# Memory keys computed during the modulation, and half of the modulation summed on TensorE

## The reference, cut to what matters

```
mod = silu(c) @ ada_w + ada_b            # ada_w: 1024 x 3072; shift, scale, gate
h = rms_norm(x, norm_g) * (1 + scale) + shift
p = h @ w_in                             # RWKV-7 branch and sparse attention follow
x = x + gate * (merged @ w_o); x = rms_norm(x, final_g)
```

```
x = x + rmsnorm(y @ w_out, mix_post_g)           # end of the mixture
h = rmsnorm(x, mem_pre_g)
mem_n = rmsnorm(mem, mem_kv_g)                   # depends on inputs alone
q = h @ w_mq;  k, v = split(mem_n @ w_mkv)       # w_mkv: 1024 x 2048
o = softmax(q k^T / 16) v                        # 4 heads of 256
x = x + rmsnorm(o @ w_mo, mem_post_g)
```

## Time and profile before

| | us |
|---|---|
| median of 3 runs | 1289.8 (1287.19 to 1291.56) |
| the profiled execution | 1291.93 |
| its span in the trace | 1290.1 |

### The profile page before, as it was taken

The page is one execution under the profiler, slowest core; times in us unless marked ns, Lnnn a source line. Parts: engine busy times, 40 slices in busy tenths (PEclk is TensorE's granted clock), DMA queues, the critical chain, the costliest instruction groups (busy, mean ns, idle before and its releaser), DMA issues.

```text
span 1290.1 us, 21180 instructions
## 1 busy us (share of the span) xinstructions
PE 1180.9 (92%) x8372; PEld 997.0 (77%) x8372; DVE 467.7 (36%) x833; ACT 593.4 (46%) x869; POOL 905.7 (70%) x913
## 2 busy tenths in 40 slices
PE   2998999999898999998999888989889999999997
PEld 2898987776677888787978867777669877888785
DVE  6476436744443111004246565331333133111101
ACT  2464133236435454435444346644465444544533
POOL 0688434434495888885999985679779756888784
PEclk9999799999999999999999999999899999999999
DMA  9656223333454666554655443436546534666562
GB/s 334 195 146 172 62 67 101 114 99 99 161 166 148 182 192 180 179 182 113 184 145 147 134 145 100 147 104 191 174 135 183 162 98 147 182 185 187 164 197 97
DMA packets 182915, 196.76 MB, mean 153 GB/s; under 512 B 7416, under 2 KB 141856, under 8 KB 182688
## 3 DMA queue, kind: packets, MB, share of 16 engines
q1 hardware_dynamic: 178336, 186.62, 48.2%
q10 hardware_dynamic: 4480, 8.78, 2.1%
HBM read 194.31 MB, written 1.06 MB: 151 GB/s over the span
## 4 chain that ended last, share of the span: by engine, by line
PE 72%; POOL 9%; DVE 8%; issue 5%; ACT 5%; DMA 2%; POOLq 0%; ACTq 0%; SPq 0%; DVEq 0%
PE ps L633 20%; PE ps L635 19%; PE ps L634 19%; PE ps L630 11%; POOL wlo L2493 9%; PE ps L638 3%; DMA raw<-in_ada_w 1%; ACT whi L1225 1%; DVE hE L1746 1%; DVE gt L1746 1%; ACT L1225 1%; DVE x L1754 1%; DVE acc L1754 0%; DVE gab L1746 0%; ACT gt L1225 0%
## 5 line engine op out<-in xcount | busy, mean ns | idle before, releaser
L2493 POOL TENSOR_TENSOR wlo<-raw,whi 128x256 fp32r<-128x256 f32 (+1 forms) x904 | 900.2, 1028 | 369.2 <-ACT whi L1225 365.4
L1225 ACT ACTIVATE whi<-raw 128x1024 fp32r<-128x1024 f32 x325 | 341.4, 1056 | 317.6 <-PE ps L635 296.8
L633 PE MATMUL ps<-whi,hThi 128*128 128x512 f32 (+2 forms) x672 | 269.4, 401 | 10.8 <-POOL wlo L2493 5.2
L635 PE MATMUL ps<-whi,hTlo 128*128 128x512 f32 (+2 forms) x672 | 260.6, 388 | 0.0
L634 PE MATMUL ps<-wlo,hThi 128*128 128x512 f32 (+2 forms) x672 | 260.0, 387 | 0.0
L633 PE MATMUL ps<-hThi,whi 128*128 128x256 f32 x576 | 171.1, 297 | 11.5 <-issue 4.6
L634 PE MATMUL ps<-hTlo,whi 128*128 128x256 f32 x576 | 164.7, 286 | 0.0
L635 PE MATMUL ps<-hThi,wlo 128*128 128x256 f32 x576 | 164.5, 286 | 0.0
L633 PEld LDWEIGHTS ps<-whi,hThi 128*128 128x128 f32 x672 | 128.1, 191 | 40.5 <-issue 13.3
L635 PEld LDWEIGHTS ps<-whi,hTlo 128*128 128x128 f32 x672 | 128.3, 191 | 26.7
L634 PEld LDWEIGHTS ps<-wlo,hThi 128*128 128x128 f32 x672 | 128.5, 191 | 21.9
(11 more groups left out here) (364 smaller groups left out, 1542.1 us busy)
## 6 DMA issues: line engine op xcount, KB each, us to landing
raw<-in_w_in SPq DMA_DIRECT2D x121, 512.0 KB, 3.6
raw<-in_ffn_w_in SPq DMA_DIRECT2D x176, 256.0 KB, 3.1
raw<-in_ffn_w_down SPq DMA_DIRECT2D x44, 512.0 KB, 3.6
raw<-in_ada_w SPq DMA_DIRECT2D x24, 512.0 KB, 5.3
raw<-in_w_mkv SPq DMA_DIRECT2D x16, 512.0 KB, 3.7
raw<-in_w_o SPq DMA_DIRECT2D x8, 512.0 KB, 3.6
raw<-in_w_branch_a SPq DMA_DIRECT2D x8, 512.0 KB, 3.7
raw<-in_w_branch_b SPq DMA_DIRECT2D x8, 512.0 KB, 3.7
```

Source lines behind the costliest of these rows:

```text
L633: e.matmul(o, l[0], r[0], start=start, stop=False)
L635: return e.matmul(o, l[1], r[0], start=False, stop=stop)
L1225: return e.activation(o, i, f, **k)
L2493: p = e.tensor_tensor(wlo[c % NHL][:, o], raw[i % NRAW][:, o], whi[c % NHL][:, o], ALU.subtract)
```

## The change

The start is laid out anew. The memory is loaded first of all, with the first 132 columns of the constants (`NA`: identity and `eps`); the rest of `con` is loaded by ACT's queue in `small`, after the first activations, and `off` shrinks from 7 x 128 to 64 columns. The modulation's slabs go in pairs: slab s below 8 (shift, n = 0, 1) is summed by DVE as before, slab s + 8 (scale) by PE straight from the raw buffer (`mod_part`: 16 float32 matmuls of 64 stationary columns and one moving column each, accumulated in PS[7] after a matmul with zeros). After the first pair comes the norm of the memory (`keynorm`) into `mT`, then the key slabs: five of them one by one before the pairs 3 to 7, three after `hfirst`. So the order of the slabs is a0 a8 K0 a1 a9 a2 a10 a3 a11 K1 a4 a12 K2 a5 a13 K3 a6 a14 K4 a7 a15 K5 K6 K7, and x is loaded ahead of the eleventh. For the first four keys ACT and POOL round only one slab ahead of PE. The normed memory (2 x 1 MB) is stored to DRAM from ACT's queue after pair 4, the keys (1 MB, collected in `qabs`) after the unit `k0`; both come back late, the memory into `oa` before `wout`, the keys into `kb` where the memory itself was loaded before. `memnorm` and the eight key slabs go from the late part; `mv0` takes their place beside `mixend`, with ten idle matmuls behind it, and only `mv1` stands beside `memlog`. The idle matmuls of the start (5 for each slab after the tenth, and 12) are gone.

```diff
+for _n, _w in [("ident", 128), ("eps", 4), ("flip", 128), ("strict", 128), ("incl", 128), ("zero", 128), ("causal", 128),
+               ("ones64", 128), ("four", 1), ("off", 64), ("pair", 5 * 64), ("eye", 64), ("low", 5 * 16), ("eye32", 32), ("reset", 256), ("one", 256),
+               ("hot", 384)]:
...
+NA = CON["flip"][0]
...
+    put("off", (s % 64 // 2 == col // 2) & (s % 2 == 0) & (col % 2 == 1))
...
-        for n in range(4):
-            for kh in range(4):
-                self.slab([(None, ada[256 * kh:256 * kh + 256, 512 * n:512 * n + 512].rearrange("(k p) n -> p k n", p=P))],
-                          (2, 512), True)
-                do("ada", 4 * n + kh)
-            if n % 2 == 1:
-                do("mod", n // 2)
-            if n == 2:
+
+        def modulate(s):
+            n, kh = divmod(s, 4)
+            self.ada[s] = self.slab([(None, ada[256 * kh:256 * kh + 256, 512 * n:512 * n + 512]
+                                      .rearrange("(k p) n -> p k n", p=P))], (2, 512), True)
+            do("ada", s)
+
+        def key_slab(c):
+            w = rows["w_mkv_2"][:, 128 * c:128 * c + 128]
+            return self.slab([(None, w.rearrange("(k p) n -> p k n", p=P))], (8, 128))
+
+        def key(c, i=None):
+            self.unit("fm", key_slab(c) if i is None else i, f"mk{c // 2}", "key", c // 2 * 2, "m", 0,
+                      j=c % 2, last=c % 2 == 1, ahead=2 if c < 4 else 3)
+
+
+        for i in range(8):
+            if i >= 3:
+                key(i - 3, early if i == 3 else None)
+            modulate(i)
+            modulate(i + 8)
+            if i == 0:
+                early = key_slab(0)
+                do("keynorm")
+            if i == 4:
+                do("load", "m_store")
+            if i == 6:
                 do("xnorm")
-        do("busy", 12, "main")
+        do("mod")
         do("hfirst")
+        for c in range(5, 8):
+            key(c)
...
+                do("load", "key_store")
...
-        do("start", "memnorm")
+        do("load", "memx")
         for n in range(2):
             tm(f"wout{n}", rows["w_out_2"], [(512 * n, 512)], "post", ("mix", n, "gt"), gen=4)
             if n == 0:
                 k = max(i for i, d in enumerate(self.todo) if d[0] == "unit" and d[1].grp == "wout0" and d[1].kh == 1)
                 self.todo.insert(k + 1, ("finish", "toh2"))
-        do("finish", "memnorm")
         do("start", "mixend")
-        for j in range(4):
-            fm(f"mk{j}", rows["w_mkv_2"], 256 * j, 256, "copy", ("kb", 2 * j), "oa", 2)
+        tm("mv0", rows["w_mkv_2"], [(1024, 512)], "tmcopy", ("vb", 0), "oa", 2)
+        do("busy", 10)
         do("finish", "mixend")
         do("load", "memrow")
         for j in range(4):
             fm(f"mq{j}", rows["w_mq_2"], 256 * j, 256, "scaled", ("qb", 2 * j, 1.0 / 16), gen=5)
         do("start", "memlog")
-        for n in range(2):
-            tm(f"mv{n}", rows["w_mkv_2"], [(1024 + 512 * n, 512)], "tmcopy", ("vb", n), "oa", 2)
+        tm("mv1", rows["w_mkv_2"], [(1536, 512)], "tmcopy", ("vb", 1), "oa", 2)
...
+        mT = [M1("mThi", [P, 8, 256], F32R), M1("mTlo", [P, 8, 256], F32R)]
+        xn0, tmp0, acc = M1("xn0", [P, 2, 1024]), M1("tmp0", [P, 8, 256]), M1("acc", [P, 2, 512])
...
+                e.dma_start(x[:, :, :], I["x"].rearrange("a (t p) d -> p (a t) d", p=P)).then_inc(S["const"].tick("first", by=16), 16)
+
+            before = {10: first}
+            summed = [plan.ada[s] for s in range(8)]
+            for t in range(2):
+                e.dma_start(gtm[:, t, 0:1024], I["mem_2"][0, 128 * t:128 * t + 128, :]).then_inc(
+                    S[f"mem{t}"].tick("in", by=16), 16)
+                if t == 0:
+                    e.dma_start(vec[:, :], vecs).then_inc(S["vecs"].tick(by=16), 16)
+                    e.dma_start(con[:, 0:NA], consts[:, 0:NA]).then_inc(S["vecs"].tick("vecs", by=16), 16)
             for i, (parts, shape, _) in enumerate(slabs):
                 if i in before:
                     before[i]()
                 old = i - NRAW
                 if old >= 0:
                     if slabs[old][2]:
-                        w.wait_ge(S["ada" if old < 16 else "mm"], ("use", old))
+                        w.wait_ge(S["ada" if old in summed else "mm"], ("use", old))
...
+                    if (u.lhs, u.gen) == ("oa", 2):
+                        w.wait_ge(S["mem_x"], "x")
+                    else:
+                        w.wait_ge(S["lhs"], (u.lhs, u.gen, kk, t))
...
+            def mod_sum():
+
+                w.wait_ge(S["ada"], ("block", 1))
                 for f in range(8):
-                    m = mm(b[:, 8 * n + f:8 * n + f + 1], acc[:, 2 * n + f // 4, f % 4 * 128:f % 4 * 128 + 128], ones1[:, :])
-                m.then_inc(S["pre_pe"].tick(("mod", n)), 1)
+                    m = mm(PS[7][:, f:f + 1], acc[:, f // 4, f % 4 * 128:f % 4 * 128 + 128], ones1[:, :], False, False)
+                m.then_inc(S["pre_pe"].tick("mod"), 1)
+
+            def mod_part(s):
+
+                i = plan.ada[s]
+                n, kh = divmod(s, 4)
+                w.wait_ge(S["ada"], "cs")
+                w.wait_ge(S["raw", i % NRAW], i)
+                r = view(raw[i % NRAW], slabs[i][1])
+                if s == 8:
+                    owner[7] = ("pre_v", "hsc")
+                    mm(PS[7][:, 0:16], vec[:, 0:128], zero16[:, :], True, False)
+                for k in range(2):
+                    kk = 2 * kh + k
+                    for q in range(4):
+                        for p0 in (0, 64):
+                            m = mm(PS[7][p0:p0 + 64, 4 * n + q:4 * n + q + 1], r[:, k, q * 128 + p0:q * 128 + p0 + 64],
+                                   cs[:, kk:kk + 1], False, (s, k, q) == (15, 1, 3))
+                m.then_inc(S["mm"].tick(("use", i), ("mod", s)), 1)
...
-                elif what == "ada" and d[0] > 9:
-                    w.wait_ge(S["ada"], ("use", d[0]))
-                    keep_busy(5, "main")
+                elif what == "ada" and d[0] >= 8:
+                    mod_part(*d)
+                elif what == "ada" and d[0] == 7:
+                    mod_sum()
+                elif what == "keynorm":
+                    norm_turn("key", gtm[:, :, 1024:2048], ("norm_a", ("key", "x", 1)), ("norm_v", ("key", "x", 1)))
...
+            def key_norm():
+                for t in range(2):
+                    w.wait_ge(S[f"mem{t}"], "in")
+                    act(gtm[:, t, 1024:2048], gtm[:, t, 0:1024], ACT.Square, accum_out=st[:, 2 + t:3 + t]).then_inc(
+                        S["norm_a"].tick(("key", "sq", t)), 1)
+                w.wait_ge(S["norm_a"])
+                act(st[:, 2:4], st[:, 2:4], ACT.Sqrt, scale=1.0 / 1024, bias=C("eps", 0, 1)).then_inc(
+                    S["norm_a"].tick(("key", "sqrt")), 1)
+                w.wait_ge(S["norm_v"], ("key", "r"))
+                for t in range(2):
+                    act(gtm[:, t, 1536:2048], gtm[:, t, 512:1024], ACT.Copy, scale=st[:, 2 + t:3 + t]).then_inc(
+                        S["norm_a"].tick(("key", "x", t)), 1)
+                round_slabs(1)
                 for f in range(0, 8, 2):
-                    h_pair("memnorm", oa, f, "mem_kv_g_2", free_h("oa", 1))
-                    yield
+                    h_pair("key", mT, f, "mem_kv_g_2", [])
...
-                    round_slabs(place[u.slab] + NHL)
+                    round_slabs(place[u.slab] + u.ahead)
...
+                w.wait_ge(S["m_out"], "out")
...
+                w.wait_ge(S["k_out"], "out")
...
+            def m_store():
+                w.wait_ge(S["lhs"], ("m", 0, 7, 1))
+                for z, d in zip(mT, m_dram):
+                    e.dma_start(d, z[:, :, :].rearrange("p f t -> p (f t)").bitcast(F32)).then_inc(S["m_out"].tick("out", by=16), 16)
+
+            def key_store():
+                w.wait_ge(S["ev_v"], ("mk3",))
+                e.dma_start(key_dram, qabs[:, :, :].rearrange("p f t -> p (f t)")).then_inc(S["k_out"].tick("out", by=16), 16)
+
             def small():
+                e.dma_start(con[:, NA:NC], consts[:, NA:NC]).then_inc(S["small"].tick(by=16), 16)
...
+                w.wait_ge(S["k_out"], "out")
                 w.wait_ge(S["split_a"], ("ob", 7))
                 w.wait_ge(S["lhs"], ("oa", 1, 7, 1))
-                e.dma_start(tmv("kb"), I["mem_2"].rearrange("a (t p) d -> p (a t) d", p=P)).then_inc(S["mem"].tick("mem", by=16), 16)
+                e.dma_start(Z["kb"][:, :, :].rearrange("p f t -> p (f t)"), key_dram).then_inc(S["mem_k"].tick("k", by=16), 16)
+
+            def memx_load():
+                w.wait_ge(S["m_out"], "out")
+                for s, key in free_h("oa", 1):
+                    w.wait_ge(S[s], key)
+                for z, d in zip(oa, m_dram):
+                    e.dma_start(z[:, :, :].rearrange("p f t -> p (f t)").bitcast(F32), d).then_inc(S["mem_x"].tick("x", by=16), 16)
...
-                    round_slabs(1)
...
-                    round_slabs(NHL)
...
```

(27 more changed lines are left out.)

83 lines of the change are left out of this document (31 added, 52 removed).

## The result

The changed kernel takes 1305.47 us (median of 4 runs, 1300.75 to 1308.65), the kernel before beside it 1288.49 (4 runs, 1286.35 to 1291.56): a ratio of 1.0114, interval 1.0083 to 1.0145. It is slower by 17 us; 1286.6 was forecast, and the range ended at 1300. The profiled execution took 1308.65 us, the longest of the four; its span is 1306.8, 16.7 more than before.

The account below looks back on a forecast made before the run. PE, busy 92% of the span, bounds the kernel; DMA and DVE hold its start. Late gain 25.6 and start loss 22.4 give -3.2: 1291.9 becomes 1288.7, or 1286.6 for the median. Range 1273 to 1300.

Parts of the forecast that it names:

- the first weights start at 70.8 ... 22.4 us later than 48.4: Start: first weights (w_in) begin on PE at 70.8, warm, 22.4 us later than the 48.4 before.
- -25.6 + 22.4 = -3.2: Whole kernel: late gain 25.6 us against start loss 22.4; the profiled execution's 1291.9 becomes 1288.7.
- 12.3 us for two turns of the loop, 6.2 a turn: Start, key slabs: from buffer return through landing, rounding, PE and next part-sum, 12.3 us for two turns.
- the low-clock rival: Start: PE's short bursts between waits stay at low clock; 15 us if all, 8 if half (1294.6); chance 0.25.
- the clock stays low in the start: Start: key matmuls and part-sums run at 1.2 GHz; price 15 us, or 8 if half (1294.6); chance 0.25.
- The store was not free beside SP's loads: Start: the 2.1 MB store shares DMA engines with SP's loads; free of it, start 1 to 2 us earlier.
- my +22.4: Start: delay of the first weights from added modulation, memory norm and key work, 48.4 to 70.8.
- The late part: 937.5 to 1052.4 us: gains of 5.9, 8.4 and 11.3, together 25.6 us (16.8 to 29.7).
- step (b): 967.6 to 994.4 us: eight key slabs go, four value slabs and ten fillers come; gain 8.4 (5.8 to 11.7).
- The cover gives out late: Late part, rival: next norm takes 2.6 us more and softmax chain 2.4 more; 5 us, 1291.6; chance 0.10.
- the upper bound of +37: Start: the low clock bounds the first weights' delay from above at +37; bytes bound it below at +6.

## Why the prediction was wrong

**The step that failed is "the first weights start at 70.8 ... 22.4 us later than 48.4".** It was +36.2. The sum -25.6 + 22.4 = -3.2 became -24.5 + 36.2, less 1.4 that the next stretches gave back, plus 6.4 in the middle: +16.7, as the spans say.

**The term inside it is "12.3 us for two turns of the loop, 6.2 a turn".** Keys 1 and 3 were forecast to end on PE at 33.7 and 46.5. They ended at 38.6 and 57.0: 9.2 us a turn. Two things in it are shown by a run of their own. One is DVE's copy of the key pair ahead of the next sum: moved, it gave 5.5 us at w_in beside the first trace, 3.0 beside the second, 4.5 to 5.4 at slab 20. I had written that DVE stands in the memory's norm, but had put the keys' eviction on no queue; I had asked what stands behind a waiting instruction for the norm and not for the copy. The other is the low clock, on keys 1 and 3, a part-sum, the transposes and keys 4 and 7: the filled gaps gave 5.6 or 3.2 us at w_in, 5.3 to 6.2 at slab 20. The store (2.9 or 0.5 us at w_in, nothing at slab 20) and the order of the second slab (1.6 or nothing) are not clear of what two traces of one kernel differ by. Together the four gave 12.0 of the 13.8 us at w_in, less than the sum of 15.6 beside the first trace, since each uncovers some of the others; 9.6 beside the second. At slab 20 they gave 6.8 to 7.7.

**One price in the loop was misread.** The part-sum was put at 1.9 us high and 3.6 low, from 1.78 us near 150 us. But the granted clock there (149.5 to 151.4 us) is 0.50, so that row was already the low level. Measured are 1.10 high and 1.88 low. The error ran against the miss: each part-sum cost less than forecast, or the same, and the price of the low-clock rival had 1.7 us for each where 0.8 is right.

**The rival "the clock stays low in the start" held in its mechanism,** with price 8 to 15 and chance 0.25. Its place and trigger were right: short bursts of matmuls, each behind a wait. Filling the gaps gave 5 to 6 us by slab 20 and 7.4 in the median. But the clock alone does not make +17 us: with the gaps filled the kernel is still slower than before, by 1.0039 (1.0017 to 1.0061). The Trainium skill, TensorE: Matmul & The Clock Gate, "HAM oscillation", says that an array that waits longer for a tile than it computes on it falls back each time; keys 1 and 3 at 0.21 us after gaps of 4.80 and 3.52 us agree, and so does the run with fillers, where key 1, its gap filled, is at 0.12, and key 2 begins low after 3.91 us.

**The store was not free beside SP's loads,** as forecast with 1 to 2 us; by how much is not clear of noise (2.9 or 0.5 us at w_in, 2.9 or 1.9 at the add). The Trainium skill, DMA: Bandwidth & Descriptors, "Issuing engines are not separate DMA queues", has all queues share 16 engines. The traces agree: beside the store that ACT issues at 36.12, key slab 3 on SP takes 6.5 us from issue to rounding, and 5.1 with the store elsewhere. Moved behind the keys, the store costs the slabs there the same way.

**The start as a place to hide work was judged wrongly at the root.** PE did nothing there for 20 us, and I let keys fill that hole. But the hole was DMA's and DVE's time, and each key and the norm bring bytes and DVE work of their own into the chain that makes the hole. The runs price it: 21.6 for the norm with its transfers, 22.9 for the keys, against 7.1 won by PE's half and the later tables. That is 37.4 in the medians, and 34.0 by slab 20 (first trace); my +22.4 had 12 to 15 of it hidden.

**The late part was right,** by step: 6.5 (5.9), 7.2 (8.4) and 10.8 (11.3). The norm's second square, the point that step (b) turned on, lies 10.7 us into its stretch at 1013.04, where it lay 11.6 us in before:

```profile
1013.04 1.04 ACT L1274 ACTIVATE gt<-x 128x1024 f32<-128x1024 f32 x1
```

The late part alone, -23.5 us in the median, confirms it. "The cover gives out late" did not come.

**The range** ended at 1300, below the upper bound of +37 that the text itself had worked out for the start. +36.2 came, but that the two agree is chance: the bound was the forecast with 15 us of low clock on it, and filling the gaps gave 5 to 6; the rest is the copy and what no single edit took away.

**Open.** Both traces of the kernel after have low stretches near 340, 818 and 880 us. The first and the third have shorter counterparts before (near 303 and 842). The last two lie where 4.0 of the 6.4 us in the middle are lost. They do not need the changed start: the kernel with the late part alone, whose start is unchanged, has them too (near 783 and 844) and loses 4.1 us in the same place. Nor do fillers decide it: the run with fillers and the one with the later copy have not got the first of the two, the one with x's norm sooner has both. The mean clock is no measure of it either: three of the four executions of the kernel without keys had 0.964 to 0.968, and two of these were faster than the one at 0.981. What brings these stretches in one kernel and not in another is not settled. Nor is it settled what, beyond the four edits, holds the start where it is.

## What to carry to other kernels

An idle engine at the start of a kernel is no room for its work, if what it waits for is a chain of transfers and another engine: price each moved step by what it puts on that chain (bytes, and the queue of the engine that copies its result out) before counting the idle time. For every new eviction ask which engine does it, what it waits for, and what stands behind it there. And work that comes in short bursts between waits, as the keys did here, is to be priced at the low clock.

## What the runs showed of the hardware

Weight loads of 64 columns with one moving column take 1.88 us for 32 at the 1.2 GHz level and 1.10 at 2.4: even with one moving column this form takes 1.7 times as long at the low level. The printed clock can hide this: in the start of the kernel without keys the 32 took 1.87 us in a stretch printed as 1.00 (from 20 to 40 us).

Two executions of one program differ by as much as most edits here are worth: the kernel after took 1308.65 us at a mean granted clock of 0.967 and 1300.75 at 0.974. The mean clock does not always go with the time: the kernel without keys took 1281.02 at 0.981 and 1277.07 at 0.968.

A store on ACT's queue delays loads on SP's: with 3 MB of stores issued from 78.64 us on, DMA moved 382 GB/s from 80 to 90 us and PE then stood 3.07 us.
